# Normalising a two-block transformer layer by token tile, with the gains as a row and half slabs in between

## The chip, the cores and the metric

The kernel runs on one core of a Trainium2 chip. The metric is the device time of one execution in microseconds (us). The engines are TensorE (PE in the profile; PEld is its weight load), VectorE (DVE), ScalarE (ACT), GpSimd (POOL) and SyncE (SP, which here only issues DMAs).

## The reference

256 tokens of width 1024 go through two blocks in float32. What the change touches are the places between the large products:

```python
h = rmsnorm(x, ln1);  z = h @ w_in            # then three attentions, gated and merged
x = x + merged @ w_o
x = x + (silu(a) * b) @ w_down                # a, b from causal_dwconv(rmsnorm(x, ln2) @ w_up)
x = rmsnorm(x, ln_f)
h = rms_norm(x, g[0]);  p = h @ w_in_first    # then convolution and recurrence
x = x + rms_norm(y_mix @ w_out, g[1])
y = memory_cross_attention(rms_norm(x, g[2]), mem_n, wq, wkv, wo)
x = x + rms_norm(y, g[3])
y = swiglu(rms_norm(x, g[4]), w_gu, w_down)
x = x + rms_norm(y, g[5])
def rms_norm(x, g): return x * rsqrt(mean(x * x) + 1e-6) * g
```

Each of these norms needs the end of the product ahead of it, and the next product needs the norm.

## The kernel before

**Slabs.** All weights come as 126 slabs of 128 x 2048 floats (1 MB), in a fixed order of stages (`STAGE_SLABS`), through a ring of four buffers `raw` that SyncE fills. Each slab is split into two parts of reduced precision: ScalarE copies `raw` to `w_hi` (L457), VectorE subtracts to get `w_lo` (L876). Activations are split in the same way (`hT_hi`, `hT_lo`), and a product is three matmuls, hi by hi, lo by hi and hi by lo (`three`, L1507 to L1509). `features` multiplies a slab of 256 output features: two groups of 128 features (`c`), eight pieces `k` of the depth, three matmuls, each with 256 tokens as its moving columns, so 48 matmuls for a slab. Its result goes to PSUM bank 0 or 1 in turn and is evacuated by ScalarE. `token_products` accumulates 256 x 1024 outputs over a stage in banks 4 to 7; token tile 0 (tokens 0 to 127) ends half a slab ahead of tile 1.

**The order** of every engine is written out by hand in one block for each engine, with semaphores between them; `splits(n)` in a block means: split all slabs up to n now.

**A norm** of x has these steps. ScalarE squares a tile of 128 tokens and sums (`sumsq`, L470), then takes the root (L476), for which a table of functions is loaded where another one was in use. VectorE inverts (L906) and scales the tile (`normed`, L913). When both tiles are there, TensorE transposes them in two portions of eight 128 x 128 blocks (`transposes`, L1537), into two PSUM banks that are used twice. ScalarE (`fill_normed`, L489) evacuates 128 x 256 at a time with the norm's gain as a scale per partition, VectorE (L924) makes the low part. The second portion waits for the banks of the first. Then the first slab of the next stage starts. Five norms go this way: ln1 ahead of stage qkv, ln2 ahead of up, g0 ahead of in2, g2 ahead of wq, g4 ahead of gu2. The norms y1, y3 and y5 are of products in banks 4 to 7: `add_normed` scales (L1420) and adds to x (L1423). ln_f scales x in place (L1164). The memory slabs `mem_a` (two) and `mem_c` (one) need nothing of x and lie under the norms ln_f/g0 and y1/g2.

## Time and profile before

| | before |
|---|---|
| median of 3 runs | 943.74 us (943.54 to 943.77) |
| profiled execution: time, span | 942.55 us, 940.3 us |
| TensorE busy | 867.8 us, 92% of the span |
| VectorE busy | 568.4 us, 60% |
| ScalarE busy | 446.1 us, 47% |
| chain that ended last | PE 79%, DVE 12%, ACT 5% |
| granted TensorE clock, mean | 0.983 |

The span is what the trace covers; the profiled execution took 2.25 us more. TensorE is busy nearly all the time, so time is lost where it waits, and work added to it counts.

### The profile page before, as it was taken

What the parts mean: (1) busy time and instruction counts of PE and PEld (TensorE: products, weight loads), DVE (VectorE), ACT (ScalarE), POOL (GpSimd) and SP (SyncE); (2) the same over time, 40 slices, a digit from 0 to 9 for tenths busy, and PEclk for the clock granted to TensorE, in tenths of its full rate; (3) what the DMA queues carried; (4) which work ended last, traced back from release to release, by engine and by line L of the source; (5) the groups of instructions that cost most, each with busy time, mean ns of one, the idle gap of its engine ahead of it and who ended that gap; (6) DMA issues with size and microseconds to landing.
All of it is one profiled execution on the core that took longest, in us unless ns stands there. A gap on an engine that the chain in (4) does not pass through costs nothing.

```text
span 940.3 us, 18577 instructions
## 1 busy us (share of the span) xinstructions
PE 867.8 (92%) x7952; PEld 801.4 (85%) x7952; DVE 568.4 (60%) x686; ACT 446.1 (47%) x572; POOL 18.8 (2%) x26
## 2 busy tenths in 40 slices
PE   2999999997999999998989989997989699999996
PEld 1999989986999998887987889886967599999784
DVE  3375655475777776547589885666444555555434
ACT  4465656445655556436373402355444544444332
POOL 1100000000000000002000000000000000000000
PEclk9999999998999999999999999999999799999999
DMA  8743345444555555554533121134513355555531
GB/s 310 262 158 136 135 135 179 162 165 154 204 185 179 178 178 179 179 181 156 201 98 130 46 93 48 47 135 157 166 58 135 112 180 178 178 178 178 185 129 45
DMA packets 21100, 143.25 MB, mean 152 GB/s; under 512 B 2490, under 2 KB 2538, under 8 KB 4912
## 3 DMA queue, kind: packets, MB, share of 16 engines
q1 hardware_dynamic: 18720, 134.23, 41.5%
q0 software_dynamic: 2176, 7.27, 2.2%
q8 instruction: 50, 0.82, 0.4%
q10 hardware_dynamic: 144, 0.85, 0.2%
q14 instruction: 10, 0.08, 0.0%
HBM read 141.27 MB, written 1.07 MB: 151 GB/s over the span
## 4 chain that ended last, share of the span: by engine, by line
PE 79%; DVE 12%; ACT 5%; issue 2%; DMA 1%; SPq 0%; DVEq 0%; ACTq 0%
PE ps L1507 23%; PE ps L1509 23%; PE ps L1508 23%; DVE w_lo L876 4%; ACT w_hi L457 3%; PE ps L1859 2%; PE ps L1537 1%; PE ps L1809 1%; ACT xn L470 1%; DMA x<-in_x 1%; DVE xn L1420 1%; PE ps L2048 1%; DVE x L1423 1%; PE ps L2028 1%; DVE cacc L1189 1%
## 5 line engine op out<-in xcount | busy, mean ns | idle before, releaser
L876 DVE TENSOR_TENSOR w_lo<-raw,w_hi 128x2048 fp32r<-128x2048 f32 x126 | 289.7, 2299 | 203.6 <-ACT w_hi L457 203.6
L1507 PE MATMUL ps<-hT_hi,w_hi 128*128 128x256 f32 x1240 | 357.0, 288 | 3.7 <-DVE w_lo L876 3.7
L1508 PE MATMUL ps<-hT_lo,w_hi 128*128 128x256 f32 x1240 | 353.9, 285 | 0.0
L1509 PE MATMUL ps<-hT_hi,w_lo 128*128 128x256 f32 x1240 | 353.8, 285 | 0.0
L457 ACT ACTIVATE w_hi<-raw 128x2048 fp32r<-128x2048 f32 x126 | 240.9, 1912 | 170.7 <-PE ps L1509 169.7
L1507 PEld LDWEIGHTS ps<-hT_hi,w_hi 128*128 128x128 f32 x1240 | 240.4, 194 | 8.4 <-issue 7.2
L1508 PEld LDWEIGHTS ps<-hT_lo,w_hi 128*128 128x128 f32 x1240 | 240.1, 194 | 0.0
L1509 PEld LDWEIGHTS ps<-hT_hi,w_lo 128*128 128x128 f32 x1240 | 239.8, 193 | 0.0
L1509 PE MATMUL ps<-w_hi,gT_lo 128*128 128x512 f32 x176 | 70.0, 398 | 0.0
L1507 PE MATMUL ps<-w_hi,gT_hi 128*128 128x512 f32 x176 | 69.6, 395 | 0.1
L1508 PE MATMUL ps<-w_lo,gT_hi 128*128 128x512 f32 x176 | 69.3, 394 | 0.0
L1537 PE MATMUL ps<-masks,xn 128*128 128x128 f32 x96 | 19.4, 369 | 41.8 <-DVE xn L913 30.1
L1123 DVE SCALAR_TENSOR_TENSOR ub<-ps,pvec,ub 128x255 f32<-128x255 f32 (+1 forms) x88 | 38.4, 478 | 29.7 <-ACT ub L616 26.8
L1507 PE MATMUL ps<-w_hi,hT_hi 128*128 128x512 f32 (+2 forms) x144 | 51.6, 358 | 4.6 <-DVE w_lo L876 3.0
L1537 PEld LDWEIGHTS ps<-masks,xn 128*128 128x128 f32 x96 | 15.0, 188 | 45.5 <-DVE xn L913 16.3
L1508 PE MATMUL ps<-w_lo,hT_hi 128*128 128x512 f32 (+2 forms) x144 | 50.9, 353 | 0.0
L1509 PE MATMUL ps<-w_hi,hT_lo 128*128 128x512 f32 (+2 forms) x144 | 50.8, 353 | 0.0
L616 ACT ACTIVATE ub<-ps,pvec 128x256 f32<-128x256 f32 x44 | 22.4, 560 | 54.7 <-PE ps L1509 54.7
L1507 PEld LDWEIGHTS ps<-w_hi,gT_hi 128*128 128x128 f32 x176 | 33.0, 188 | 8.3 <-DVE w_lo L876 0.7
L1508 PEld LDWEIGHTS ps<-w_lo,gT_hi 128*128 128x128 f32 x176 | 33.0, 188 | 8.3
L1509 PEld LDWEIGHTS ps<-w_hi,gT_lo 128*128 128x128 f32 x176 | 33.0, 188 | 7.8
L1507 PEld LDWEIGHTS ps<-w_hi,hT_hi 128*128 128x128 f32 x144 | 27.2, 189 | 9.7 <-DVE w_lo L876 3.6
(277 smaller groups left out, 1040.2 us busy)
## 6 DMA issues: line engine op xcount, KB each, us to landing
raw<-in_weights SPq DMA_DIRECT2D x126, 1024.0 KB, 4.9
row_gain<-in_rows_vec POOLq DMA_DIRECT2D x4, 512.0 KB, 4.5
bias<-bias_scratch POOLq DMA_DIRECT2D x1, 1536.0 KB, 10.0
x<-in_x SPq DMA_DIRECT2D x2, 512.0 KB, 7.3
xn<-in_mem POOLq DMA_DIRECT2D x2, 512.0 KB, 4.2
out<-x SPq DMA_DIRECT2D x2, 512.0 KB, 2.6
masks<-in_masks ACTq DMA_DIRECT2D x1, 833.5 KB, 6.9
bias<-bias_scratch POOLq DMA_DIRECT2D x1, 768.0 KB, 11.6
```

Source lines behind the costliest of these rows:

```text
L457: A(w_hi[:, n % SPLIT, :], raw[:, n % RAW, :], ACT.Copy).then_inc(sems["hi_ready"], 1)
L470: A(ub[:, 1, :, :, :].rearrange("p a b n -> p (a b n)") if name == "mem" else xn[:, t, :], src(t), ACT.Square, accum_out=stat[:, 4 * q + t ...
L616: A(ub[:, p % 2, s, c, :], src[:, c * T:(c + 1) * T], ACT.Identity, bias=pvec[:, bass.ds(p + 2 * turn, 1), col + 3], scale=pvec[:, bass.ds ...
L876: V.tensor_tensor(w_lo[:, n % SPLIT, :], raw[:, n % RAW, :], w_hi[:, n % SPLIT, :].bitcast(F32), ALU.subtract).then_inc(sems["lo_ready"], 1)
L1123: ins = V.scalar_tensor_tensor(out=dst, in0=src[:, c * T:(c + 1) * T - lag], scalar=pvec[:, bass.ds(p + 2 * turn, 1), 4 * (2 * s + c) + ta ...
L1189: ins = V.scalar_tensor_tensor(out=dst, in0=src, scalar=vec[:, col:col + 1], in1=dst, op0=ALU.mult, op1=ALU.add)
L1420: do(V.scalar_tensor_tensor(out=xn[:, t, :], in0=banks(4 + 2 * t, 2), scalar=inverse_rms(name, t), in1=row_gain[:, :], op0=ALU.mult, op1=A ...
L1507: mm(dst, left[0], right[0], start=first, stop=False)
L1508: mm(dst, left[0], right[1], start=False, stop=False)
L1509: return mm(dst, left[1], right[0], start=False, stop=last)
L1537: last = nc.tensor.transpose(ps[:, transposed_bank(name, k), k % 2 * T + t * P:k % 2 * T + (t + 1) * P], xn[:, t, k * P:(k + 1) * P], ident)
L1859: last = mm(ps[to, b + q, j * CHUNK:(j + 1) * CHUNK], left[rows, 8 * q + j, :], right(rows, 8 * q + j), start=True, stop=True)
```

## The change

- The five gains are loaded by GpSimd's queue as rows that are the same on all partitions (`norm_gain`, 512 KB each), and VectorE multiplies by them while it scales x. The evacuations need no scale and take 128 x 512 at a time.
- `transposes` takes one token tile, into two banks of its own. In stages up, wq and gu2 the first slab is computed by `first_slab`: transposes of tile 0, the slab for tile 0, transposes of tile 1, the slab for tile 1. Stage qkv does the transposes of both tiles and then the same halves. In in2 the transposes of both tiles stand in the middle of the second memory slab, and the slab itself stays whole.
- x is loaded ahead of all but 131 columns of the masks, each tile has a semaphore of its own, and the first four weight slabs wait for nothing.
- `root_table` takes a root of a constant ahead of the sum of squares, so that the table is loaded there.
- `add_normed` multiplies by the gain first and then scales and adds in one instruction. In y5 that is done in halves of 512 columns, each stored by a DMA of its own.
- Around ln_f the second memory slab is split between the two tiles. GpSimd's multiplications for the convolution's taps wait for the end of stage up and not for that of down.

```diff
+                sp.dma_start(x[:, t, :], x_in[0, t * P:(t + 1) * P, :]).then_inc(sems[f"x_in_{t}"], 16)
 
             for n in range(RAW):
-                if n == 0:
-
-                    sp.wait_ge(sems["x_in"], 16 * TT)
-                if n == 1:
-                    sp.wait_ge(sems["masks_ready"], 16)
                 sp.dma_start(raw[:, n, :], weights[n]).then_inc(raw_in[n], 16)
...
-            pool.dma_start(vec[:, :], vec_in).then_inc(sems["consts_in"], 16)
+            def load_norm_gain(name):
+
+                n = 4 + NORM_GAINS.index(name)
+                pool.dma_start(norm_gain[:, :], rows_in[n].partition_broadcast(P)).then_inc(sems["norm_gain_in"], 16)
+
+            load_norm_gain("ln1")
             for src, dst in ((fb_w, fbw[:, :]), (onehot_in, onehot[:, :, :]), (table_in, table[:, :]),
                              (row_small.partition_broadcast(P), small[:, :])):
                 pool.dma_start(dst, src).then_inc(sems["small_in"], 16)
+            pool.dma_start(vec[:, :], vec_in).then_inc(sems["consts_in"], 16)
+            pool.dma_start(masks[:, MASKS_FIRST:MASK_COLS], masks_in[:, MASKS_FIRST:MASK_COLS])\
+                .then_inc(sems["more_masks"], 16)
...
-            pool.wait_ge(sems["x_ready"], X_READY["w_o"] + TT)
+            load_row_gain(0, 0)
             pool.dma_start(pvec[:, :, :], pairs_vec).then_inc(sems["pvec_in"], 16)
+            pool.wait_ge(sems["slab_used"], FIRST_SLAB["w_o"])
+            load_norm_gain("ln2")
             pool.wait_ge(sems["xt_ready"], 4 * (TRANSPOSED.index("ln2") + 1))
+            load_norm_gain("g0")
...
             pool.wait_ge(sems["late_in"], 16)
-            pool.wait_ge(sems["x_ready"], X_READY["down"] + TT)
...
                 for t in range(TT):
+                    if t and between:
...
-                      accum_out=stat[:, 4 * q + t:4 * q + t + 1]).then_inc(sems["sumsq_ready"], 1)
+                    unused = (ub[:, 1, :, :, :].rearrange("p a b n -> p (a b n)") if name == "mem" else
+                              banks(2, 2) if name[0] == "y" else xn[:, t, :])
+                    A(unused, src(t), ACT.Square, accum_out=stat[:, 4 * q + t:4 * q + t + 1]).then_inc(sems["sumsq_ready"], 1)
...
+            def fill_normed(name, tiles=range(TT)):
+
+                z = TRANSPOSED.index(name)
+                for t in tiles:
+                    for half in range(2):
+                        act.wait_ge(sems["xt_ready"], 4 * z + 2 * t + half + 1)
+                        A(hT_hi[:, 4 * half:4 * half + 4, t * P:(t + 1) * P],
+                          bank(transposed_half(t, half)).rearrange("p (k n) -> p k n", k=4), ACT.Copy)\
+                            .then_inc(sems["hT_hi_ready"], 2)
...
+            def root_table(n):
+
+                A(stat[:, 61 + n % 2:62 + n % 2], stat[:, 60:61], ACT.Sqrt)
+
+            act.wait_ge(sems["stat_set"], 1)
+            root_table(0)
+            sumsq("ln1", lambda t: x[:, t, :], lambda t: act.wait_ge(sems[f"x_in_{t}"], 16))
+            fill_normed("ln1", (0,))
             splits(0)
-            act.wait_ge(sems["consts_in"], 16)
...
+            root_table(0)
+            sumsq("ln_f", lambda t: x[:, t, :], x_tile("down"), lambda: splits(n_a + 1))
             sumsq("g0", lambda t: x[:, t, :], x_tile("ln_f"))
-            memory_out(0)
-            splits(FIRST_SLAB["in2"])
+            for i in range(MEM_A - 1):
+                memory_out(i)
+                splits(n_a + i + 2)
             fill_normed("g0")
-            for i in range(1, MEM_A):
-                memory_out(i)
+            memory_out(MEM_A - 1)
...
+            def normed(name):
 
                 for t in range(TT):
-                    V.tensor_scalar(xn[:, t, :], (x if src is None else src)[:, t, :], inverse_rms(name, t), None,
-                                    ALU.mult).then_inc(sems["xn_ready"], 1)
-
...
+            def fill_normed(name, tiles=range(TT)):
+
+                for t in tiles:
+                    for half in range(2):
+                        dve.wait_ge(sems["hT_hi_ready"], KD * FILL[name] + 4 * t + 2 * half + 2)
+                        ks, cols = slice(4 * half, 4 * half + 4), slice(t * P, (t + 1) * P)
+                        V.tensor_tensor(hT_lo[:, ks, cols], bank(transposed_half(t, half)).rearrange("p (k n) -> p k n", k=4),
+                                        hT_hi[:, ks, cols].bitcast(F32), ALU.subtract).then_inc(sems["hT_lo_ready"], 2)
...
-
 
             dve.wait_ge(sems["row_gain_in"], 16)
             for t in range(TT):
+                if t:
+                    splits(n_a + 1)
                 V.scalar_tensor_tensor(out=x[:, t, :], in0=x[:, t, :], scalar=inverse_rms("ln_f", t),
                                        in1=row_gain[:, :], op0=ALU.mult, op1=ALU.mult).then_inc(sems["x_ready"], 1)
-            do(V.memset(glu[:, :, 0:TAPS - 1], 0.0))
             normed("g0")
             splits(FIRST_SLAB["in2"])
             fill_normed("g0")
+            do(V.memset(glu[:, :, 0:TAPS - 1], 0.0))
 
...
                 for t in range(TT):
-                    do(V.scalar_tensor_tensor(out=xn[:, t, :], in0=banks(4 + 2 * t, 2), scalar=inverse_rms(name, t),
-                                              in1=row_gain[:, :], op0=ALU.mult, op1=ALU.mult))
-                    settle()
-                    V.tensor_tensor(x[:, t, :], x[:, t, :], xn[:, t, :], ALU.add).then_inc(sems["x_ready"], 1)
+                    dve.wait_ge(sems["sumsq_ready"], TT * STATS[name] + t + 1)
+                    do(V.tensor_tensor(xn[:, t, :], banks(4 + 2 * t, 2), row_gain[:, :], ALU.mult))
+                    if t and between:
+                        between()
+                    inverse = inverse_rms(name, t)
+                    for part in range(parts):
+                        cols = slice(part * D // parts, (part + 1) * D // parts)
+                        V.scalar_tensor_tensor(out=x[:, t, cols], in0=xn[:, t, cols], scalar=inverse, in1=x[:, t, cols],
+                                               op0=ALU.mult, op1=ALU.add).then_inc(sems["x_ready"], 1)
 
             splits(FIRST_SLAB["mem_c"])
...
+            def transposes(name, t):
 
                 z = TRANSPOSED.index(name)
-                pe.wait_ge(sems["xn_ready"], TT * (z + 1))
-                for k in tiles:
-                    if k >= 4 and k % 2 == 0 and name != "mem":
-                        operand(FILL[name], k - 3)
+                pe.wait_ge(sems["xn_ready"], TT * z + t + 1)
+                for half in range(2):
+                    for k in range(4):
+                        last = nc.tensor.transpose(ps[:, transposed_half(t, half), k * P:(k + 1) * P],
+                                                   xn[:, t, (4 * half + k) * P:(4 * half + k + 1) * P], ident)
...
+            def features_by_token(n, u, name, between):
+
+                bank_free(u)
+                hi, lo = slab(n)
+                for t in range(TT):
+                    if t:
+                        between()
+                    cols = slice(t * P, (t + 1) * P)
+                    for c in range(2):
+                        for k in range(KD):
+                            if c == 0 and k % 4 == 0:
+                                operand(FILL[name], 4 * t + k // 2 + 1)
+                            w = slice(k * T + c * P, k * T + (c + 1) * P)
+                            last = three(ps[:, u % 2, c * T + t * P:c * T + (t + 1) * P], (hi[:, w], lo[:, w]),
+                                         (hT_hi[:, k, cols], hT_lo[:, k, cols]), k == 0, k == KD - 1)
+                return last
+
+            def first_slab(stage, name):
+
+                transposes(name, 0)
+                used(features_by_token(FIRST_SLAB[stage], FIRST_UNIT[stage], name, lambda: transposes(name, 1)))
 
...
-                    used(features(n0 + j, u0 + j, fill if j == 0 else None))
+                first_slab(name, norm)
+                used(features(n0 + 1, u0 + 1, None))
                 with pe.Fori(0, (PAIRS - 1) // 2) as turn:
...
+            def memory_slabs(first, last, name):
+
+                for i in range(first, last):
+                    for j, _ in enumerate(memory_slab(i)):
+                        if name and i == last - 1 and j == 7:
+                            transposes(name, 0)
+                            transposes(name, 1)
+
+            memory_slabs(0, MEM_A, "g0")
...
             for i in range(11):
-                used(features(n0 + i, u0 + i, FILL["g0"] if i == 0 else None))
+                if i == 0:
+                    operand(FILL["g0"], KD - 1)
+                used(features(n0 + i, u0 + i, None))
                 if i == 2:
...
             n0, u0 = FIRST_SLAB["wq"], FIRST_UNIT["wq"]
-            for i in range(4):
-                used(features(n0 + i, u0 + i, FILL["g2"] if i == 0 else None))
+            first_slab("wq", "g2")
+            for i in range(1, 4):
+                used(features(n0 + i, u0 + i, None))
```

TensorE's order at the norm ln2, first before (the last matmuls of stage w_o, the transposes of `xn` by the identity in `masks`, the first slab of up):

```order
L1507 MATMUL ps<-w_hi,hT_hi 128x512
L1508 MATMUL ps<-w_lo,hT_hi 128x512
L1509 MATMUL ps<-w_hi,hT_lo 128x512
L1537 MATMUL ps<-masks,xn 128x128 x16
L1507 MATMUL ps<-hT_hi,w_hi 128x256
L1508 MATMUL ps<-hT_lo,w_hi 128x256
L1509 MATMUL ps<-hT_hi,w_lo 128x256
```

Then the changed kernel, around its second portion of transposes; 48 matmuls of 128 columns stand ahead of it and 48 behind:

```order
L1563 MATMUL ps<-hT_hi,w_hi 128x128
L1564 MATMUL ps<-hT_lo,w_hi 128x128
L1565 MATMUL ps<-hT_hi,w_lo 128x128
L1591 MATMUL ps<-masks,xn 128x128 x8
L1563 MATMUL ps<-hT_hi,w_hi 128x128
```

The slab's 48 matmuls of 256 columns have become 96 of 128, and eight of the sixteen transposes have moved into its middle. Wq and gu2 read the same.

VectorE's order from the end of stage down to in2, before (`x<-x,ps` adds the product, `x<-x,stat,row_gain` is ln_f, `xn` is g0):

```order
L1101 TENSOR_TENSOR x<-x,ps 128x1024 x2
L876 TENSOR_TENSOR w_lo<-raw,w_hi 128x2048
L906 RECIPROCAL stat<-stat 128x1
L1164 SCALAR_TENSOR_TENSOR x<-x,stat,row_gain 128x1024
L906 RECIPROCAL stat<-stat 128x1
L1164 SCALAR_TENSOR_TENSOR x<-x,stat,row_gain 128x1024
L1166 MEMSET glu 128x4x30
```

And in the changed kernel:

```order
L1152 TENSOR_TENSOR x<-x,ps 128x1024 x2
L939 RECIPROCAL stat<-stat 128x1
L1215 SCALAR_TENSOR_TENSOR x<-x,stat,row_gain 128x1024
L909 TENSOR_TENSOR w_lo<-raw,w_hi 128x2048
L939 RECIPROCAL stat<-stat 128x1
L1215 SCALAR_TENSOR_TENSOR x<-x,stat,row_gain 128x1024
L939 RECIPROCAL stat<-stat 128x1
L948 SCALAR_TENSOR_TENSOR xn<-x,stat,norm_gain 128x1024
```

The split of the second memory slab has moved behind the first tile of ln_f, and the memset behind the norm.

## Rows read from the trace of the kernel before

**Rows 1.** The waits of TensorE, the longest in total: us, times, longest one.

```profile
PE ps L1537 <- DVE xn L913: 30.1, 5, 15.0
```

**Rows 2.** Timeline of TensorE, slab 6 of stage qkv: start us, us, engine, line.

```profile
72.98 0.28 PE L1508 MATMUL ps<-w_lo,hT_hi 128*128 128x128 f32 x1
...
78.12 0.28 PE L1509 MATMUL ps<-w_hi,hT_lo 128*128 128x128 f32 x1
```

**Rows 3.** The same timeline, first slab of stage wq, once the clock is up.

```profile
663.11 0.28 PE L1509 MATMUL ps<-hT_hi,w_lo 128*128 128x256 f32 x1
...
667.91 0.28 PE L1507 MATMUL ps<-hT_hi,w_hi 128*128 128x256 f32 x1
```

**Rows 4.** Timeline of the start, all engines.

```profile
9.65 1.06 ACT L470 ACTIVATE xn<-x 128x1024 f32<-128x1024 f32 x1 [7.18 <-DMA x<-in_x]
...
14.70 1.91 ACT L457 ACTIVATE w_hi<-raw 128x2048 fp32r<-128x2048 f32 x1 [0.81 <-DMA raw<-in_weights]
...
24.32 0.58 PE L1507 MATMUL ps<-hT_hi,w_hi 128*128 128x256 f32 x1
...
31.87 0.60 ACT L531 ACTIVATE qkT<-ps 128x512 f32<-128x512 f32 x1 [6.59 <-PE ps L1509]
```

**Rows 5.** DMA issues from 0 to 30 us: count, size, us to landing.

```profile
x<-in_x SPq DMA_DIRECT2D x2, 512.0 KB, 7.3
...
row_gain<-in_rows_vec POOLq DMA_DIRECT2D x1, 512.0 KB, 6.7
```

**Rows 6.** Timeline around ln2; ScalarE, then VectorE, then TensorE.

```profile
222.34 1.28 ACT L476 ACT_TABLE_LOAD   x1
...
230.44 1.69 ACT L489 ACTIVATE hT_hi<-ps,vec 128x256 fp32r<-128x256 f32 x4 [1.26 <-PE ps L1537]
...
237.65 1.02 ACT L616 ACTIVATE ub<-ps,pvec 128x256 f32<-128x256 f32 x2 [3.71 <-PE ps L1509]
...
224.16 0.75 DVE L913 TENSOR_SCALAR xn<-x,stat 128x1024 f32<-128x1024 f32 x1
...
229.29 1.97 PE L1537 MATMUL ps<-masks,xn 128*128 128x128 f32 x8 [0.99 <-DVE hT_lo L924]
```

**Rows 7.** VectorE's groups, shapes apart: busy us, mean ns, idle before.

```profile
L1472 DVE TENSOR_TENSOR ub<-ub,ps 128x512 f32<-128x512 f32 x11 | 7.6, 688 | 6.7 <-PE ps L1509 6.7
```

**Rows 8.** Timeline around ln_f and g0; VectorE, GpSimd, ScalarE.

```profile
423.02 1.22 DVE L1101 TENSOR_TENSOR x<-x,ps 128x1024 f32<-128x1024 f32 x1 [0.16 <-PE ps L1509]
...
428.58 2.76 DVE L1164 SCALAR_TENSOR_TENSOR x<-x,stat,row_gain 128x1024 f32<-128x1024 f32 x1
...
431.44 1.29 DVE L1164 SCALAR_TENSOR_TENSOR x<-x,stat,row_gain 128x1024 f32<-128x1024 f32 x1
...
424.40 5.86 POOL L433 TENSOR_TENSOR stk<-masks,vec 128x992 f32<-128x992 f32 x2 [191.23 <-DVE x L1101]
...
448.45 0.84 ACT L663 ACTIVATE xn<-ps,omu 128x256 f32<-128x256 f32 x2 [3.89 <-PE ps L1509]
```

**Rows 9.** Timeline around y1 and g2; VectorE, then ScalarE.

```profile
656.25 2.29 DVE L876 TENSOR_TENSOR w_lo<-raw,w_hi 128x2048 fp32r<-128x2048 f32 x1 [1.47 <-ACT w_hi L457]
...
667.75 0.60 ACT L804 ACTIVATE q2T<-ps 128x512 f32<-128x512 f32 x1 [3.72 <-PE ps L1509]
```

**Rows 10.** Timeline of ScalarE around y3 and g4.

```profile
726.38 1.03 ACT L470 ACTIVATE xn<-ps 128x1024 f32<-128x1024 f32 x1 [0.74 <-PE ps L1509]
...
749.00 0.60 ACT L846 ACTIVATE ub<-ps 128x512 f32<-128x512 f32 x1 [2.95 <-PE ps L1509]
```

**Rows 11.** TensorE in two stretches: length, busy (instructions), granted clock, DMA.

```profile
655.00:659.00 4.00, 0.93 (x8) 1.00 0.11 42
735.00:744.00 9.00, 5.86 (x26) 0.50 0.15 58
```

**Rows 12.** Timeline of the end, ScalarE and VectorE.

```profile
929.09 1.03 ACT L470 ACTIVATE xn<-ps 128x1024 f32<-128x1024 f32 x1 [6.42 <-PE ps L1509]
...
936.08 1.22 DVE L1423 TENSOR_TENSOR x<-x,xn 128x1024 f32<-128x1024 f32 x1
```

More of the change, by code:

```diff
@@ L186, with transposed_half @@
 )
-def transposed_bank(name, k):
-    return k // 2 if name == "mem" else 2 + k // 2 % 2
+def transposed_half(t, half):
+    return 2 + 2 * t + half
 class Steps:
@@ L596, in _ @@
             splits(FIRST_SLAB["up"])
+            root_table(1)
             sumsq("ln2", lambda t: x[:, t, :], x_tile("w_o"))
@@ L1481, in _ @@
             splits(SLABS - 1)
-            add_normed("y5", "down2", 3)
+            add_normed("y5", 3, parts=2)
         @block.tensor
@@ L1718, in _, with feed_loop @@
             token_products("w_o", hT, lambda i: operand(FILL["merged"], 2 * i + 1))
-            transposes("ln2")
-            def feed_loop(name, fill):
+            def feed_loop(name, norm):
                 n0, u0 = FIRST_SLAB[name], FIRST_UNIT[name]
-                for j in range(2):
-                    used(features(n0 + j, u0 + j, fill if j == 0 else None))
+                first_slab(name, norm)
+                used(features(n0 + 1, u0 + 1, None))
                 with pe.Fori(0, (PAIRS - 1) // 2) as turn:
```

130 lines of the change are left out of this document (71 added, 59 removed).

## The prediction

> **What bounds the kernel now.** I read the chain of waits first. TensorE holds most of it, and its longest wait is for the scaled tile `xn` of the norms: 30.1 us in five places, 15.0 us of it at the start [rows 1]. So the change aims at the right places, and each can be costed from its timeline: the time from a fixed event ahead of the norm to the evacuation of the next stage's first slab. What the reader should take from the timelines is that work on TensorE counts in full behind the norm, since the slabs that follow run back to back.
>
> **The price of half slabs.** In stage qkv, slab 6 has products with 128 moving columns in the same number format: from the start at 72.98 to that at 78.12 there are 46 steps, 0.112 us each [rows 2]. With 256 columns it is 40 steps from 663.11 to 667.91, 0.120 us each [rows 3]. Halving the columns hardly shortens a matmul. A whole slab takes 48 x 0.120 = 5.8 us, in halves 96 x 0.112 = 10.7 us: 5.0 us more. The Trainium skill's page "TensorE: Matmul & The Clock Gate" says two things here. Its section "LDWEIGHTS (loading the stationary operand)" gives a load of 128 columns as 128 / 1.2 = 107 ns, which would explain the row's 112. Its section "Back-to-back issue gap" gives a sustained spacing of about 81 ns at 128 columns; by that a slab in halves would take 7.8 us and four of them 11.6 us less than I count. I go by rows 2, which is this kernel's own shape and format.
>
> **The second tile in the middle.** Its transposes are issued behind the first tile's 48 matmuls, and the next matmul needs them evacuated. With the clock at 1.2 GHz ScalarE started 1.15 us after the first four transposes of a portion did (229.29 to 230.44 [rows 6]); at 2.4 GHz about 0.7. Then a copy of 128 x 512 (0.60 [rows 9]) and a subtraction (0.69 [rows 7]), with 0.1 for hand-overs: 2.1 us in which TensorE does 0.9 us of transposes. Nothing hides this. So from the first matmul of tile 0 to the slab's evacuation it is 5.35 + 2.1 + 5.35 + 0.3 = 13.1 us at full clock, where the whole slab takes 5.8 + 0.3 = 6.1. Half slabs pay only where the first matmul comes 7 us earlier.
>
> **ln2 and up: +2.9 us.** The table load at 222.34 (1.28) goes, its cover being the stretch from the end of the last weight split to the sum [rows 6]. Then `xn` of tile 0 starts at 222.85 and not 224.16, and takes 1.29 (the three-operand form [rows 8]) and not 0.75: done at 224.15. Four transposes at full clock, copy: 225.5. VectorE is at `xn` of tile 1 until 225.65, subtraction until 226.35, first matmul at 226.4. End at 226.4 + 13.1 = 239.5. For the clock I add 1.0: after some 8 us of waiting TensorE stood at 0.50 of its clock in the stretch 735 to 744 (1.2 GHz of 2.4), and it stayed at 1.00 over an idle stretch from 655 to 659 [rows 11]; here the gap shrinks to 3.2 us, so it may go either way, and a fall costs 1.3 to 3. End 240.5 against 237.65 [rows 6].
>
> **g2 and wq: +5.6 us.** Here a memory slab lies under y1, and what ends last is the split of wq's first slab: VectorE does it at 656.25 for 2.29 us [rows 9], before any low part. It stays in front of them. ScalarE's memory copy moves behind its own split, which gives 0.4: the split ends at 658.2, first matmul at 658.95. End at 672.05, and 1.3 for the clock, since the gap ahead stays 3.6 us: 673.4 against 667.75 [rows 9].
>
> **g4 and gu2: +3.5 us.** `root_table` stands behind the split that ends at 725.64, and load and root keep ScalarE until 727.2, so y3's square of tile 0 starts 0.8 late (726.38 [rows 10]); the root behind it comes 0.45 earlier than now, and VectorE's multiplication no longer waits for the root. x of tile 0 is ready 0.85 earlier, `xn` of tile 0 at 735.3. TensorE is cold after 6 us: half the transposes until 736.5, copy, subtraction, first matmul at 737.85. End at 737.85 + 13.1 + 1.5 (15 matmuls at half speed) = 752.45 against 749.0 [rows 10]. Rearranging `add_normed` alone gives no more, as 1.22 + 1.29 remain for each tile.
>
> **ln_f, g0 and in2: -3.2 us.** No half slab here. GpSimd's multiplications (424.40, 5.86 us) stretched ln_f's first tile to 2.76 us, where the second took 1.29 [rows 8]. They move under stage down, where VectorE has over 3 us of slack in each slab; without that slack they would cost 1.5. From the addition that ends at 424.24 [rows 8]: ln_f of tile 0 until 425.95, the split until 428.65 (TensorE needs it then, as before), ln_f of tile 1 until 430.15, `xn` at 431.7 and 433.2. TensorE waits about 0.6 us in mid-slab for tile 1 and ends the slab at 437.1. VectorE splits in2's first slab until 436.45 and makes four low parts (4 x 0.69) until 439.15. Slab and evacuation 6.1: 445.25 against 448.45 [rows 8]. TensorE idles 2 us there, too short I think for the clock to fall; if it falls, 1.6 is lost.
>
> **The start: -2.6 us.** x lands at 9.6 [rows 4], 7.3 us after its issue in the middle [rows 5], with the masks beside it. Alone in front, tile 0 should be there at about 5.3. Then the gain row ends last: its like took 6.7 us [rows 5], so 7 to 8. `xn` until 9.4 and 10.8, cold transposes, ScalarE's copies of tile 0 until 12. Weight slab 0 was waited for at 14.70, because it was issued behind x [rows 4]; now about 12. Splits (1.91 and 2.3) until 16.25, first matmul at 16.3 and not 24.32 [rows 4]. Then 10.7 + 0.3 and 2.0 for the low clock at its beginning: 29.3 against 31.87 [rows 4]. Of 8 us won, the half slab takes 5 back, and here nothing stands between the halves.
>
> **The end: -1.6 us.** y5's square starts at 929.09 as before [rows 12]. Without the load, with the multiplication beside the root: tile 0 done at 933.05; tile 1, whose square starts at 931.9, multiplies until 934.3 and ends at 935.85 in halves of 0.7, where the last addition ended at 937.30 [rows 12]. The smaller last store gives 0.1 more.
>
> **Sum.** 2.9 + 5.6 + 3.5 - 3.2 - 2.6 - 1.6 = +4.6 us. The profiled execution took 942.55 us (span 940.3), 1.2 under the median of 943.74, so I put the sum on the median: 948.3 us. The other parts cost nothing: gain rows are loaded tens of us ahead, and the rest of the masks is wanted first at 46 us or later.
>
> **Rivals.**
> 1. *It cancels.* The clock stays up in ln2 and g2 (-2.3), weight slab 0 lands at 10.5 (-1.5), ends of chains overlap better by 0.4: +0.4, so 944.1 us. For it speaks the 1.00 in [rows 11]; against it that g2's gap is as long as the one behind which the clock fell. 0.2.
> 2. *Narrow matmuls are cheaper between long waits than rows 2 say, and it gets faster.* Bounds are 0.060 (half of 0.120) and 0.112; in the middle, at 0.086, four slabs save 4 x 96 x 0.026 = 10.0 us: 938.3 us. It decides from 0.100 down. Against it: 46 steps at 0.112 without one shorter. The page's 81 ns would give 948.3 - 11.6 = 936.7. 0.09.
> 3. *The start waits for something else*, such as the small constants or the masks' first part behind 5 MB of weights, and the clock costs two periods in three places: about +4 more, 952.3 us. 0.1.
> 4. *Start and end win more than I see*, by over 6.5 us in all: 941.5 us. 0.05.
>
> **Numbers.** The forecast has 0.56, with a range of its own from 945.8 to 950.5. About 0.2%, 1.9 us, is what a measurement can tell from no change. Slower: forecast and rival 3, with little of the forecast's edge lost, 0.66. Same: rival 1 and that edge, 0.2. Faster: rivals 2 and 4, 0.14. The range has to reach rivals 1 and 3 and a little beyond: 942.3 to 952.
>
> **What would show it.** Right: the 128-column matmuls of `hT` at 0.112 us, slab ends at about 240.5, 673 and 752 shifted by what went before, TensorE idle over 1 us in the middle of three slabs, its busy time up by some 20 us, first slab at 16.3, final addition 1.5 us nearer to the last matmul. Wrong: a shorter spacing; a first matmul of tile 0 more than 5 us earlier in up, wq or gu2; a start that gains over 5 us.

## The result: 4.7% slower, and the profile after

The changed kernel took 988.73 us (median of 4 runs, 986.81 to 989.57), the kernel before 943.75 in the same session: ratio 1.0473, interval 1.0455 to 1.0491. The sign was forecast; the size was not, +45 us where +4.6 was expected. The profiled execution took 988.13 us, span 986.3, with a mean granted clock of 0.94 against 0.983.

From the page of the changed kernel: its busy line, the busy share of TensorE in 40 slices, and the granted clock in the same slices (in tenths):

```profile
PE 924.1 (94%) x8144; PEld 860.7 (87%) x8144; DVE 567.7 (58%) x669; ACT 440.3 (45%) x557; POOL 21.3 (2%) x32
...
PE   4999999998999999999989889998989799999997
...
PEclk8699999997799999999999999997799579999999
```

TensorE is the busier for it, not the idler: the time went into busy slices, in which the clock line dips four times. The groups of TensorE with shapes apart (busy us, mean ns of one, idle before) say which matmuls these are:

```profile
L1563 PE MATMUL ps<-hT_hi,w_hi 128*128 128x256 f32 x1176 | 339.5, 289 | 5.3 <-DVE w_lo L909 3.7 <-issue 1.6
...
L1563 PE MATMUL ps<-hT_hi,w_hi 128*128 128x128 f32 x128 | 53.0, 414 | 9.3 <-DVE hT_lo L957 7.9 <-DVE w_lo L909 1.4
L1564 PE MATMUL ps<-hT_lo,w_hi 128*128 128x128 f32 x128 | 52.8, 412 | 0.0
```

The half slabs' 384 matmuls took 412 to 414 ns each, where one of twice the width took 289 and one of 128 columns 280 in [rows 2]. Three stretches of the changed kernel, from first to last half of the slabs of ln2, wq and gu2, and behind two of them the next slab (length, busy and count, granted clock, DMA):

```profile
234.70:257.60 22.90, 22.21 (x104) 0.50 0.36 131
257.60:265.00 7.40, 7.40 (x50) 0.76 0.13 21
677.00:701.00 24.00, 22.66 (x105) 0.51 0.28 93
701.00:708.50 7.50, 7.50 (x50) 0.74 0.21 56
772.00:796.00 24.00, 22.59 (x105) 0.50 0.13 45
```

The clock stood at 0.50 (1.2 GHz) for all of these three half slabs. The timeline of TensorE at the seam of the first and the next slab shows it come back only there:

```profile
257.47 0.41 PE L1565 MATMUL ps<-hT_hi,w_lo 128*128 128x128 f32 x1
257.69 0.52 PE L1563 MATMUL ps<-hT_hi,w_hi 128*128 128x256 f32 x1
...
260.78 0.41 PE L1565 MATMUL ps<-hT_hi,w_lo 128*128 128x256 f32 x1
260.99 0.34 PE L1563 MATMUL ps<-hT_hi,w_hi 128*128 128x256 f32 x1
261.17 0.28 PE L1564 MATMUL ps<-hT_lo,w_hi 128*128 128x256 f32 x1
```

Starts lie 0.213 us apart up to 260.99, and soon 0.120. A slab in halves therefore took 96 x 0.213 = 20.5 us, not 10.7. In the kernel before, the clock came back inside the slab (the spacing 0.120 of [rows 3] begins 2 us into it). The start, on VectorE, TensorE and ScalarE:

```profile
9.62 1.28 DVE L948 SCALAR_TENSOR_TENSOR xn<-x,stat,norm_gain 128x1024 f32<-128x1024 f32 x1 [3.28 <-DMA norm_gain<-in_rows_vec]
...
17.86 0.33 PE L1563 MATMUL ps<-hT_hi,w_hi 128*128 128x128 f32 x1 [1.45 <-DVE w_lo L909]
...
18.70 0.34 PE L1564 MATMUL ps<-hT_lo,w_hi 128*128 128x128 f32 x1
18.83 0.42 PE L1565 MATMUL ps<-hT_hi,w_lo 128*128 128x128 f32 x1
19.05 0.41 PE L1563 MATMUL ps<-hT_hi,w_hi 128*128 128x128 f32 x1
...
37.85 0.60 ACT L559 ACTIVATE qkT<-ps 128x512 f32<-128x512 f32 x1 [18.76 <-PE ps L1565]
```

The first matmul starts at 17.86, 6.5 us ahead of [rows 4]. Eight matmuls are 0.111 us apart; then the clock falls with the engine busy, the others are 0.213 apart, and the slab ends 6 us behind [rows 4]. Around ln2, ScalarE and TensorE:

```profile
257.93 1.02 ACT L646 ACTIVATE ub<-ps,pvec 128x256 f32<-128x256 f32 x2 [8.74 <-PE ps L1565]
...
232.19 1.09 PE L1591 MATMUL ps<-masks,xn 128*128 128x128 f32 x8 [3.11 <-DVE xn L948]
234.49 0.45 PE L1563 MATMUL ps<-hT_hi,w_hi 128*128 128x128 f32 x1 [1.20 <-DVE hT_lo L957]
```

The wait ahead of the transposes is 3.11 us (5.23 before, at 226.34). The norm's own part is shorter. What follows the first matmul takes 23.4 us to its evacuation where 13.1 was forecast.

The waits of TensorE, to set beside [rows 1]:

```profile
PE ps L1591 <- DVE xn L948: 20.4, 4, 11.1
...
PE ps L1563 <- DVE hT_lo L957: 7.9, 6, 3.8
```

The whole by stages, each as the time from one evacuation on ScalarE to the next (the second slab of qkv, up, wq and gu2, and the first of in2), from the timeline of one execution of each kernel. Columns e1 to e12 belong to experiments below.

| us | before | after | e2 | e1 | e3 | e4 | e11 | e12 |
|---|---|---|---|---|---|---|---|---|
| start to qkv | 37.6 | 45.8 | 52.1 | 33.6 | 32.7 | 34.0 | 29.0 | 30.7 |
| to up | 205.8 | 219.4 | 221.5 | 203.0 | 205.8 | 207.6 | 203.7 | 202.3 |
| to in2 | 205.0 | 200.9 | 205.3 | 201.5 | 200.9 | 200.9 | 200.9 | 200.9 |
| to wq | 225.1 | 242.5 | 242.2 | 224.6 | 228.7 | 233.4 | 227.5 | 225.2 |
| to gu2 | 87.0 | 101.1 | 101.7 | 84.1 | 87.2 | 88.4 | 84.4 | 83.4 |
| to the end | 179.8 | 176.6 | 179.8 | 176.7 | 176.7 | 176.6 | 176.7 | 176.7 |
| span | 940.3 | 986.3 | 1002.7 | 923.4 | 931.9 | 941.0 | 922.1 | 919.2 |

Against before the changed kernel lost 8.2, 13.6, 17.5 and 14.1 us in the four stages with a half slab and won 4.1 and 3.1 in the two others. Of the 17.5, 15.6 lie in the last 100 us, around y1, g2 and wq, and the rest in stages ahead of them that the change leaves as they are.

### The profile page after: what moved, and what is told of

It is laid out like the page before. It is cut to its first block, busy times and chain, and to the rows that moved or that the text cites. A ratio compares the mean times of both kernels' runs of the same rounds, so it can differ in the third digit from the quotient of the medians.

```text
span 986.3 us, 18987 instructions
## 1 busy us (share of the span) xinstructions
PE 924.1 (94%) x8144; PEld 860.7 (87%) x8144; DVE 567.7 (58%) x669; ACT 440.3 (45%) x557; POOL 21.3 (2%) x32
## 4 chain that ended last, share of the span: by engine, by line
PE 81%; DVE 10%; ACT 4%; issue 3%; DMA 1%; DVEq 0%; ACTq 0%; POOLq 0%
PE ps L1563 24%; PE ps L1565 23%; PE ps L1564 23%; DVE w_lo L909 4%; ACT w_hi L468 2%; PE ps L1955 2%; PE ps L1903 1%; DMA norm_gain<-in_rows_vec 1%; PE ps L1591 1%; PE ps L2142 1%; PE ps L2122 1%; DVE xn L948 1%; DVE cacc L1240 1%; PE ps L1721 1%; PE ps L1865 0%
## 5 line engine op out<-in xcount | busy, mean ns | idle before, releaser
L1563 PE MATMUL ps<-hT_hi,w_hi 128*128 128x256 f32 (+1 forms) x1304 | 392.5, 301 | 14.6 <-DVE hT_lo L957 7.9
L1564 PE MATMUL ps<-hT_lo,w_hi 128*128 128x256 f32 (+1 forms) x1304 | 389.6, 299 | 0.0
L1565 PE MATMUL ps<-hT_hi,w_lo 128*128 128x256 f32 (+1 forms) x1304 | 389.4, 299 | 0.0
L1563 PEld LDWEIGHTS ps<-hT_hi,w_hi 128*128 128x128 f32 x1304 | 272.1, 209 | 21.0 <-issue 14.3
L1564 PEld LDWEIGHTS ps<-hT_lo,w_hi 128*128 128x128 f32 x1304 | 272.1, 209 | 0.0
L1565 PEld LDWEIGHTS ps<-hT_hi,w_lo 128*128 128x128 f32 x1304 | 272.1, 209 | 0.0
L1591 PE MATMUL ps<-masks,xn 128*128 128x128 f32 x80 | 15.7, 364 | 20.4 <-DVE xn L948 20.4
L957 DVE TENSOR_TENSOR hT_lo<-ps,hT_hi 128x512 fp32r<-128x512 f32 x20 | 13.2, 687 | 36.6 <-ACT hT_hi L511 36.6
```

What stands on the lines that cost most here:

```text
L957: V.tensor_tensor(hT_lo[:, ks, cols], bank(transposed_half(t, half)).rearrange("p (k n) -> p k n", k=4), hT_hi[:, ks, cols].bitcast(F32), ...
L1563: mm(dst, left[0], right[0], start=first, stop=False)
L1564: mm(dst, left[0], right[1], start=False, stop=False)
L1565: return mm(dst, left[1], right[0], start=False, stop=last)
L1591: last = nc.tensor.transpose(ps[:, transposed_half(t, half), k * P:(k + 1) * P], xn[:, t, (4 * half + k) * P:(4 * half + k + 1) * P], ident)
```

## Experiments

Theory A: a slab in 128-column matmuls that begins at 1.2 GHz, or falls to it, stays there to its end. Theory B: halves cost the forecast 5 us each, and the rest is new waits. Theory C: the low clock comes from the changed waits, whatever the width. e2, e3, e4, e6 and e10 were each timed in a single execution, the others in four or five.

### e1: the change without its half slabs

```diff
                 transposes(name, 0)
-                used(features_by_token(FIRST_SLAB[stage], FIRST_UNIT[stage], name, lambda: transposes(name, 1)))
+                transposes(name, 1)
+                operand(FILL[name], KD - 1)
+                used(features(FIRST_SLAB[stage], FIRST_UNIT[stage], None))
```

> The changed kernel with the first slabs of qkv, up, wq and gu2 whole again (48 matmuls of 256 columns, after the transposes of both tiles); all else as changed. Theory A (a slab of 128-column matmuls that begins at 1.2 GHz stays there to its end, so it takes about 20.5 us and not 10.7): all of the loss is in the halves, and what is left of the change gains; from the starts of the slabs in the changed kernel's trace about 925 us (920 to 930). Theory B (halves cost 5 us each as I counted, the other 25 us are new waits elsewhere): 988.7 - 20 = about 969 us. Theory C (the low clock comes from the changed waits ahead of the slabs, not from the columns): 965 to 975 us with the granted clock at 0.50 for over 10 us behind each norm.

Measured: 925.46 us (924.67 to 926.38), ratio 0.981 (0.9787 to 0.9832). That is A's number, and 63 us below the changed kernel. The rest of the change is worth 18 us and makes the kernel faster. The wait ahead of ln2's transposes is that of the changed kernel (3.11 us in both), and the clock returns, which speaks against C. TensorE over ln2 in e1:

```profile
216.00:220.00 4.00, 0.89 (x4) 0.90 0.79 262
220.00:224.00 4.00, 3.11 (x16) 0.67 0.01 2
224.00:228.00 4.00, 3.26 (x27) 1.00 0.78 228
```

Here it is back at 222.6 us, ahead of the slab's first matmul at 224.74: it rose while the norm's sixteen fp32 transposes ran in a row, thirteen of them in the 2.83 us from 219.77 at a granted clock of 0.50. In wq it came back inside the slab, which begins at 649.35 and has a granted clock of 0.50 up to 652.7 and of 1.00 behind. e3 shows the latter with the changed kernel's order.

### e2: half slabs alone, in the kernel before

```diff
-                    used(features(n0 + i, u0 + i, FILL["ln1"] if i == 0 else None, between=between))
+                    used(features_by_token(n0, u0, FILL["ln1"]) if i == 0 else
+                         features(n0 + i, u0 + i, None, between=between))
```

and the same for the first slabs of up, gu2 and wq, both tiles being ready when the slab begins.

> The kernel before with one edit: the first slabs of qkv, up, wq and gu2 in halves of 128 columns, behind both tiles' transposes, nothing between the halves. Theory A: 20.5 us in place of some 6.7 and up to 2 more at low clock in the next slab, so about 14.5 us in each of four places: about 1002 us. Theories B and C: 5 us in each of four places: about 963 us.

Measured: 1004.89 us, 61 above before; A expected 1002. B and C, which expected 963, fall, since no wait was changed. TensorE over the first slabs of up, wq and gu2:

```profile
244.00:265.80 21.80, 21.80 (x104) 0.50 0.31 113
693.00:713.60 20.60, 20.60 (x99) 0.50 0.23 87
789.00:809.80 20.80, 20.80 (x100) 0.50 0.14 51
```

### e3: order by tile, but 256 moving columns

The tile's activations become the stationary operand and the weights move, 24 matmuls a tile in place of 48. The results of the four slabs lie transposed, so what follows works on other numbers, at the same sizes.

```diff
...
-                            last = three(ps[:, u % 2, c * T + t * P:c * T + (t + 1) * P], (hi[:, w], lo[:, w]),
-                                         (hT_hi[:, k, cols], hT_lo[:, k, cols]), k == 0, k == KD - 1)
...
+                        w = slice(k * T, (k + 1) * T)
+                        last = three(ps[:, u % 2, t * T:(t + 1) * T], (hT_hi[:, k, cols], hT_lo[:, k, cols]),
+                                     (hi[:, w], lo[:, w]), k == 0, k == KD - 1)
```

> The changed kernel with its order of tiles, but each half slab as 24 matmuls in which 256 columns of weights move and the activations of 128 tokens stand (the result of these four slabs lies with tokens on the partitions and is not the reference's). Theory A: the clock comes up as in the kernel before, and no work is added: within 3 us of the whole slabs, 922 to 928 us. Theory B: 20 us less than changed, 969 us. Theory C: 965 us or more.

Measured: 933.74 us (ratio of the two kernels' medians to e1: 1.009). The width explains 55 of the 63 us. But A's 922 to 928 was missed by 6 us. Against e1 the order by tile costs 2.8 us in up and 3.1 in gu2 and wins 0.9 at the start. Of the 4.1 us up to wq, 2.3 lie in a stage that no edit touches and where e3's clock was low from 532 to 540 us, and 1.7 at wq. In ln2 the slab begins at 221.90 with the clock at 0.50, in the changed kernel's order (3.11 us of waiting ahead of the transposes in both, 0.78 behind them against 1.20), and with 256 columns the clock comes back inside it, which theory C had excluded:

```profile
221.90:225.40 3.50, 3.50 (x16) 0.50 0.00 0
225.40:228.40 3.00, 2.04 (x18) 1.00 0.00 0
```

In each of the three places TensorE waits between the tiles, here in wq:

```profile
655.92 1.03 PE L1591 MATMUL ps<-masks,xn 128*128 128x128 f32 x8
658.06 0.39 PE L1563 MATMUL ps<-w_hi,hT_hi 128*128 128x256 f32 x1 [1.10 <-DVE hT_lo L957]
```

How much of it is clock and how much order, e11 tells apart.

### e4: the changed kernel with a warm TensorE

Unused matmuls fill the waits ahead of the first tile's products; nothing reads their results.

```diff
...
+                for _i in range(n[0]):
+                    mm(ps[:, FIRST_UNIT[stage] % 2, :], hi[:, 0:P], hi[:, 0:512], start=True, stop=True)
                 transposes(name, 0)
+                for _i in range(n[1]):
+                    mm(ps[:, FIRST_UNIT[stage] % 2, :], hi[:, 0:P], hi[:, 0:512], start=True, stop=True)
```

`n` is (14, 4) in ln2, (0, 16) in g2 and (24, 4) in g4. At the start four fp32 ones go ahead of the first transposes and six fp32r ones behind them.

> The changed kernel with extra matmuls of 512 columns into a free PSUM bank while TensorE waits ahead of the half slabs (14 and 4 at ln2, 16 at g2, 24 and 4 at g4, 4 and 6 at the start), so that the halves begin at 2.4 GHz; their results are not used. Theory A in its simple form (the level at the start of the halves decides): halves at 0.112 us, about 948 us, which is my prediction. If halves pull the clock down by themselves even from 2.4 GHz, the time stays between 960 and 989 us. Theory B: about 988 us, no change.

Measured: 942.9 us (span 941.0): 46 us back, with the same 384 narrow matmuls. So they stay at 2.4 GHz when they begin there. First the hi-by-hi products of up's halves (32 of the 96 matmuls, from 216 to 236 us), then TensorE in wq's second half:

```profile
L1563 PE MATMUL ps<-hT_hi,w_hi 128*128 128x128 f32 x32 | 8.9, 277 | 1.4 <-DVE hT_lo L957 1.4
...
659.70:661.70 2.00, 1.91 (x17) 1.00 0.00 0
661.70:668.70 7.00, 7.00 (x35) 0.50 0.44 150
```

In up the mean is 277 ns, at 2.4 GHz. In wq the second half, too, began at 2.4 GHz, behind a wait of 1.1 us between the tiles; the clock fell 1.9 us into it, and some 31 of its 48 matmuls ran at 1.2 GHz. Behind the same wait of 1.10 us in up it stayed up. But for these 31, this kernel is the forecast's own world, half slabs at full clock, and it came out level with before (940.3 to 941.0 in span) where the forecast said +4.6.

### e5 and e12: e1 with a warm TensorE

```diff
...
+                fillers(n[0])
                 transposes(name, 0)
-                used(features_by_token(FIRST_SLAB[stage], FIRST_UNIT[stage], name, lambda: transposes(name, 1)))
+                fillers(n[1])
+                transposes(name, 1)
+                fillers(n[2])
+                operand(FILL[name], KD - 1)
+                used(features(FIRST_SLAB[stage], FIRST_UNIT[stage], None))
```

The fillers are unused fp32 matmuls of 256 columns; `n` is (6, 0, 4) in ln2, (0, 0, 9) in g2 and (12, 0, 4) in g4. At the start there are four fp32 ones ahead of the transposes and twelve fp32r ones behind.

> The kernel of e1 (norms by tile, whole first slabs, 925.46 us) with unused matmuls in the waits: 4 fp32 of 512 columns at the start and 12 of 512 behind the first transposes, then fp32 ones of 256 columns (6 and 4 in ln2, 9 in g2, 12 and 4 in g4). Theory A (a slab begun at 1.2 GHz loses time, one of 256 columns some 3.4 us of it at half speed, so 1.7 us; one of 128 columns its whole length): up to 1.7 us less at the start, in up, wq and gu2 and 1 us less in the transposes of ln2 and g4, 5 to 8 us in all: 917 to 920 us. Rival: in whole slabs the wait ends with VectorE's last low part whatever the clock is, and fillers that end late give it back: 924 to 927 us.

> The kernel of e5 once more, beside e11 on the same chip and in five rounds, since the two are to be told apart by a few us: 920 to 923 us by both theories.

Measured: 921.43 us (ratio 0.9763, 0.9741 to 0.9785), and again 921.15 in five rounds (0.9744, 0.973 to 0.9757). Theory A's 917 to 920 was a little too low, the rival's 924 to 927 too high. In e5's profiled execution the start gains 3.0 us over e1, wq 1.3 in the last 100 us up to it, and gu2 0.8. (The stage to wq as a whole is no shorter than e1's, since 1.8 us were lost ahead of that, in slabs that no edit touches.) It is the fastest kernel of the study, 67 us below the changed one; the results of 51 matmuls in it are not used.

### e7, e8, e9: parts of the 18 us

e7 takes out the five later calls of `root_table`; e8 puts SP's two waits ahead of the weights back; e9 puts the taps back beside ln_f:

```diff
-            root_table(1)
```

```diff
+                if n == 0:
+                    for t in range(TT):
+                        sp.wait_ge(sems[f"x_in_{t}"], 16)
+                if n == 1:
+                    sp.wait_ge(sems["masks_ready"], 16)
```

```diff
-            pool.wait_ge(sems["g_lo_ready"], PAIRS)
+            pool.wait_ge(sems["x_ready"], X_READY["down"] + TT)
```

> The kernel of e1 without the early loads of the root table (all calls of root_table but the first are gone; the load then comes with the first root of each norm). Its ln2, g4 and end stages came 2.8, 2.8 and 3.2 us shorter than before, g2 0.5. Theory P: the load of 1.28 us is on the path in ln2, y3 and y5 and is what the early load takes off: 925.46 + 3 x 1.28 = 929.3 us, and 930.6 if ln_f's counts too. Rival Q: the gains come from the work by tile (VectorE's tile 0 beside ScalarE's tile 1), the load is hidden: 925.5 to 926.5 us.

> The kernel of e1 with SP's waits of the kernel before put back: weight slab 0 is issued when x has landed, slab 1 when the first masks have. The first slab's evacuation was at 27.8 us in e1 and 31.9 before. Theory P: the 4.0 us of the start come from weight slab 0 landing early, so with x at some 4.5 us and slab 0 then landing near 9.7, behind the gain row at 9.6, little is lost: 925.5 to 926.5 us would say that x alone in front is the gain. Rival Q: the weights' early issue is what pays, 2 us or more are lost: 927.5 us or more.

> The kernel of e1 with GpSimd's multiplications of the taps where they were before, beside ln_f. Stage ln_f to in2 came 3.6 us shorter in e1 than before. Theory P: GpSimd's work stretched VectorE's instruction from 1.29 to 2.76 us and what follows, and moving it gave 1.5 of the 3.6 us: 927.0 us. Rival Q: the stage is bound by the order of the splits, the multiplications cost nothing: 925.5 us. Rival R: they cost all of the 3.6: 929 us.

Measured: 930.48 us (930.24 to 931.65), 928.19 (924.31 to 931.6) and 930.45 (928.5 to 932.02). None of the three totals can be read as the price of its edit. Each kernel shows places where the clock stays low longer than in e1, also where nothing was edited; in ln2, up to the second evacuation, e8 and e9 took 205.1 and 204.8 us where e1 took 203.0, with equal waits. TensorE of e8 over ln2, to set beside e1's:

```profile
216.00:220.00 4.00, 0.89 (x5) 0.83 0.80 260
220.00:224.00 4.00, 3.36 (x16) 0.50 0.01 4
224.00:228.00 4.00, 3.09 (x14) 0.50 0.74 187
228.00:232.00 4.00, 4.00 (x32) 0.89 1.03 423
```

So the parts are read from their own rows. e7: ScalarE loads the table behind the sum of tile 0, and TensorE waits 4.39 us ahead of ln2's transposes, 1.28 more than in e1, the whole load:

```profile
217.21 1.28 ACT L490 ACT_TABLE_LOAD   x1
...
220.37 3.57 PE L1586 MATMUL ps<-masks,xn 128*128 128x128 f32 x16 [4.39 <-DVE xn L943]
```

Ahead of g4 the same wait is 5.53 against 5.81, so the early load gains nothing there, as the forecast had it; at the end it is worth 0.4. e8: the first qkv slab is evacuated at 27.57 us, against 27.84 in e1. The early issue of the weights was worth nothing: with x alone in front, slab 0 is split at 14.06, as in e1 (14.10), where the splits had been held up by the norm. And the norm was held up by the gain row, which lands 2.1 us later beside the early weights: VectorE's first `xn` begins at 10.14 in e1 and at 8.05 in e8. e9: GpSimd's multiplications are back at 417.30, and VectorE shows them:

```profile
417.66 2.65 DVE L1215 SCALAR_TENSOR_TENSOR x<-x,stat,row_gain 128x1024 f32<-128x1024 f32 x1
...
420.24 4.01 DVE L909 TENSOR_TENSOR w_lo<-raw,w_hi 128x2048 fp32r<-128x2048 f32 x1
...
424.35 1.28 DVE L1215 SCALAR_TENSOR_TENSOR x<-x,stat,row_gain 128x1024 f32<-128x1024 f32 x1
```

Two instructions take 1.4 and 1.7 us more than their like. From ln_f's first tile to in2's first evacuation e9 takes 22.62 us, where e1 and all others with the change take 19.86 to 19.88: 2.7 us is the price there, more than theory P's 1.5 and less than R's 3.6. Another 0.7 us comes back in stage down, which no longer has the multiplications beside it (62.25 us from its first to its last matmul; 62.98 in the changed kernel). That makes 2.1 us net against the 200.9 of most kernels in the table. Against e1 the stage is only 1.5 longer, since e1's own stage down took 63.60 us without an edit there: that this hits P's 1.5 is luck. In the profiled executions e9 is 6.7 us behind e1; the rest lies mostly in ln2, wq and gu2 (1.8, 1.7 and 2.7 us), where its clock stayed low longer.

### e6 and e10: streams by width, behind the kernel

Eight copies on ScalarE keep TensorE waiting 8.6 us or longer, then it gets a stream without waits, every matmul with its weight load.

```diff
+                for count, widths in stream:
+                    for i in range(count):
+                        at, n = i % 8 * P, widths[i % len(widths)]
+                        last = mm(ps[:, 0, 0:n], w_hi[:, 0, at:at + P], w_hi[:, 1, 0:n], start=True, stop=True)
```

> The kernel of e1, and behind its last addition six streams of unused fp32r matmuls, each with a weight load of its own and each begun after some 8 to 10 us in which TensorE waits for eight copies of ScalarE: 144 matmuls of 128 columns; of 160; of 192; of 256; 24 of 512 columns and then 144 of 128; 144 of 128, 24 of 512, 72 of 128. Theory A (a dense stream of 128 columns doesn't bring the clock back, wider ones do): the first stream at 0.213 us throughout (30.7 us), the fourth at 0.213 us for about 3.5 us and then 0.120; 160 and 192 tell where between them it turns; the fifth at 0.112 us to its end; in the sixth 0.213 until some 3.5 us into the 512-column ones, then 0.112 for the last 72. Rival: it was the half slab's alternation, its banks or its waits, and not the columns: the first stream rises after some 3.5 us like the fourth.

> As e6, with five other streams: 320 matmuls of 128 columns; 144 alternating 128 and 256; 144 of 64; 144 of which every fourth has 512 columns and the others 128; 144 of 144 columns. Theory A: the first stays at 0.213 us for all of its 68 us, the 64-column one too; the alternating one and the one with a 512 in four rise some 3.5 to 7 us in. Rival (the clock comes back with time, narrow streams are only slower at it): the first rises somewhere in its 68 us.

Measured, e6's groups behind the last addition, then e10's (read up to 1150 us, where nine matmuls of its last stream were still to come):

```profile
L2175 PE MATMUL ps<-w_hi 128*128 128x160 f32 x144 | 31.0, 416 | 8.6 <-ACT ps L902 8.6
L2175 PE MATMUL ps<-w_hi 128*128 128x256 f32 x144 | 19.5, 302 | 8.6 <-ACT ps L902 8.6
L2175 PE MATMUL ps<-w_hi 128*128 128x192 f32 x144 | 18.1, 292 | 8.6 <-ACT ps L902 8.6
```

```profile
L2175 PE MATMUL ps<-w_hi 128*128 128x64 f32 x144 | 30.9, 401 | 8.6 <-ACT ps L902 8.6
L2175 PE MATMUL ps<-w_hi 128*128 128x144 f32 x135 | 29.1, 416 | 8.6 <-ACT ps L902 8.6
```

The same number of matmuls takes 31.0 us with 160 columns and 18.1 with 192: the wider ones are done sooner. The clock in four-us stretches of e6, first in its stream of 128 columns (933.97 to 964.9), then behind 24 wide ones, then around the 24 wide ones in the middle of the last stream:

```profile
958.00:962.00 4.00, 4.00 (x21) 0.50 0.02 4
...
1086.00:1090.00 4.00, 4.00 (x39) 1.00 0.00 0
...
1126.00:1130.00 4.00, 4.00 (x21) 0.50 0.00 0
1130.00:1134.00 4.00, 4.00 (x15) 0.62 0.02 4
...
1138.00:1142.00 4.00, 4.00 (x39) 1.00 0.00 0
```

128-column products stand at 0.50 or at 1.00, by what ran ahead of them. In e10, 320 of 128 columns held 0.50 for all of their 68 us, so the rival "it comes back with time" falls too; 64 and 144 columns never rose; alternating 128 and 256 rose after some 4 us. One expectation failed: a stream in which every fourth has 512 columns stayed at 0.50 for its 38 us. Why that mix doesn't lift the clock is open. All these streams are of the products' own format, fp32r; e1's fp32 transposes, also of 128 columns and also with a weight load each, ran at the same pace (thirteen in 2.83 us) and did see the clock come back. So width alone doesn't decide it, and no run separates the formats.

### e11: order by tile, 256 columns and a warm TensorE

> The kernel of e3 (tile order, first slab as 24 matmuls a tile with 256 moving weight columns, 933.74 us) with unused matmuls in the waits ahead of the first tile's products, as in e4 and e5. It asks whether the order by tile inside the first slab pays at all once neither width nor clock stands in its way. Theory D (it doesn't: the wait between the tiles and VectorE's low parts take what the earlier first matmul gives): 921 to 927 us, no faster than e5's 921.4. Rival: it pays its 1 to 2 us at each of the four places: 914 to 918 us.

The edits are those of e3 and of e5 together, with somewhat fewer unused matmuls ((6, 2) in ln2, (0, 8) in g2, (12, 2) in g4, and six behind the first transposes). Measured: 925.94 us (0.979, 0.9776 to 0.9803) beside e12's 921.15 (0.9744, 0.973 to 0.9757). The times are those that theory D expected: with neither width nor clock in the way, products by tile inside the slab are still 4.8 us slower. In the profiled executions, 2.9 us apart, they win 1.7 us at the start, where nothing stands between the tiles, and lose 1.4, 1.5 and 1.1 us in up, wq and gu2; the rest lies in stages without an edit.

D's reason is only a part of it. In each of these three places 1.0 us is lost in the *second* slab, of which nothing was edited: TensorE waits for its low weights, a wait that e12 doesn't have there.

```profile
226.64 0.36 PE L1563 MATMUL ps<-hT_hi,w_hi 128*128 128x256 f32 x1 [0.77 <-DVE w_lo L909]
```

ScalarE and VectorE have the split of the second slab behind tile 1's copies and low parts, and these now come in mid-slab (in up, VectorE splits the second slab at 224.20 in e11 and at 222.06 in e12, though e11's first slab begins 3.5 us earlier, at 217.65). A split placed ahead of tile 1 might give this back; no run tried it. So that the order by tile loses by itself is not shown, only that it does with the splits where they are.

## Why the prediction was wrong

**The bound and the places: right.** TensorE held the end, the norms' waits were the target, and [rows 1]'s 30.1 us of waits for `xn` fell to 20.4.

**The price of half slabs: right at 2.4 GHz, wrong as the price here.** This is the step that failed. The forecast took 0.112 us from [rows 2], whose matmuls stood in a stream that already ran at 2.4 GHz, and added 2.0, 1.0, 1.3 and 1.5 us in the terms "start", "ln2 and up", "g2 and wq" and "g4 and gu2" for a low clock "at its beginning". It assumed that the clock comes back inside a half slab as it did inside a whole one. It doesn't: 96 x (0.213 - 0.112) = 9.7 us each, then 1.5 to 2.2 us in the next slab, in which the clock comes back, and in three places slower transposes between the halves (1.93 us in place of 1.04). That is some 12 us a place where 1.0 to 2.0 were allowed. e4, where some 31 of wq's 96 matmuls still ran slow, measures it directly, in one execution: 988.73 - 942.9 = 45.8 us for the clock. [rows 11] had shown the 0.50 behind g4's wait; what it couldn't show was a narrow stream at that level, and the forecast gave that unseen case no rival; rival 3, the only one with a costlier clock, put some 4 us on the clock and the start together. The forecast also read [rows 11]'s 1.00 from 655 to 659 as a wait that the clock had outlasted. It fell right behind that stretch: from 659.2 to 662.6 the kernel before stands at 0.50.

The Trainium skill ("TensorE: Matmul & The Clock Gate", section "What's actually happening") calls the warm-up a matter of time and not of the number of matmuls, with everything after it at 2.4 GHz, and has a 128-column kernel among its examples. No run here agrees with that for fp32r streams that reload weights for every 128 columns: e10's stayed at 1.2 GHz for 68 us. For e1's fp32 transposes the trace agrees, and for e6's streams of 192 and 256 columns. Its section "Back-to-back issue gap" (81 ns) stood beside rival 2. No row here is that short: 0.111 to 0.112 us in this kernel at 2.4 GHz, 0.108 in e6's streams. The same page's section "LDWEIGHTS (loading the stationary operand)", 107 ns a load, is the one that the trace bears out.

**The terms at full clock, by e4.** Against before, without the clock's part:

| term | forecast | e4 | 
|---|---|---|
| start | -2.6 | -3.6 |
| ln2 and up | +2.9 | +1.9 |
| ln_f, g0, in2 | -3.2 | -4.1 |
| g2 and wq | +5.6 | +8.4 |
| g4 and gu2 | +3.5 | +1.4 |
| end | -1.6 | -3.1 |
| sum | +4.6 | +0.7 |

wq is the one that still holds matmuls at 1.2 GHz. ln2 and gu2 come out 1 to 2 us better than forecast, for the forecast's clock allowance of 1.0 and 1.5 isn't paid there.

**The start: the gain near in size, the cause half right.** x landed at 4.6 us (forecast 5.3). The gain row did end last, but at 9.62 and not at 7 to 8: e8 shows that the early weight slabs beside it cost it 2.1 us. The first matmul came at 17.86 and not 16.3. Weight slab 0 was counted as a gain; e8 shows it worth nothing. Without the 2.0 us set aside for the clock the forecast is a gain of 4.6, and e4 has 3.6.

**Second tile in the middle: right in kind.** Tile 1's products wait 1.1 us for VectorE's low part in e3 and e4. At full clock that, and the second slab's late split, is what e11 pays.

**GpSimd's taps: right in kind** (1.29 us for each part of ln_f in the changed kernel, 2.76 for the first in [rows 8]; e9 turned it back). The forecast held them free under stage down; e9 shows 0.7 us paid there.

**The end: right by its own chain.** From y5's square to the last addition it is 8.21 us before (929.09 to 937.30) and 6.65 after (977.25 to 983.90): -1.56. The last store takes 0.6 us less, not 0.1, and another 1.0 us is won between gu2's second slab and the last product. It lies in the last stage's 264 matmuls of 512 columns, which take 61.70 us from first to last in before and e2 and 60.65 in all kernels with the change; why, no run shows.

## What to carry to other kernels

Before a matmul is narrowed, look at the granted clock where the narrow ones will *begin*, and price them at that level: a spacing taken from the middle of a stream at 2.4 GHz holds only there. To begin at 2.4 GHz is no guarantee behind a wait: at the start of the changed kernel the clock fell 0.8 us into the narrow slab and did not come back in it. Keep the first slab behind a long wait wide, and put narrow work behind wide work; where a wait can't be shortened, unused wide matmuls in it were worth 4 us here and 46 in e4. And before a reordering is thrown out, take it apart: 18 us of gain lay under a loss of 63.

## What the runs showed of the hardware that was not expected

- A stream without waits of fp32r matmuls of 64, 128, 144 or 160 columns, each with a weight load, that began at 1.2 GHz stayed there: 0.213 us apart for as long as it lasted, 68 us at most. Streams of 192 and 256 rose to 2.4 GHz, where 110 and 103 of them fit in 12 us. One of 128 that began at 2.4 GHz kept it (74 in 8 us).
- The clock also fell inside a busy narrow stream: 0.8 us after its first matmul, behind a wait of 1.45 us (18.8 in the changed kernel), and 1.9 us after it, behind a wait of 1.1 us between two narrow halves (e4, wq). In e4's up it stayed at 2.4 GHz behind the same 1.1 us.
- Sixteen fp32 transposes in a row, each 128 columns with a weight load, begun at 1.2 GHz, did see it rise: 2.8 us after the first of them (e1, ln2).
- Ahead of its first change in a trace the granted clock can read 1.00 when it isn't: in e2 it does so from 24 to 44.5 us, where 97 matmuls take 20.5 us, 0.211 each. There the spacing has to be read.
- While GpSimd multiplied, VectorE's split of 128 x 2048 took 4.01 us in place of 2.29 (e9).
- How long the clock stays low behind the same wait differs between kernels that are equal there (e1 and e8 in ln2: by their rows some 3.4 us at 1.2 GHz, and some 10). That alone moves a stage by some 2 us (203.0 to 205.1), e8's four executions spread over 7 us, and single edits of this size can't be read from totals.
